# First local-attention layer: keys projected once per head, rope partners by DMA, head sums as two rounded products

## The chip, the cores and the metric

One core of a Trainium2 chip runs the whole program. The metric is the device time of one execution, in microseconds (us); a kernel's number is the median of its runs. The time of the kernel before is 2983.45 us, the median of 3 runs (2982.0 to 2984.66).

## The reference, cut to what matters

The program computes two small networks one after the other on 512 positions of width 1024: a local-attention layer and an RWKV layer, each followed by a gated feed-forward layer, and then a block with three attention branches (called a, b and c in the kernel) and a last feed-forward layer. What the change touches is how queries and keys are made:

```python
def rms_norm(x, g):
    y = xf * lax.rsqrt(jnp.mean(xf * xf, axis=-1, keepdims=True) + NORM_EPS)
    return (y * g.astype(F32)).astype(x.dtype)

# first local layer: 16 query heads, 4 key heads, 4 value heads of 64 columns
qkv = h @ w_qkv
q = rope_slice(rms_norm(q, q_gain), cos, sin, 0)   # norm over each head's 64 columns
k = rope_slice(rms_norm(k, k_gain), cos, sin, 0)   # then columns 0-7 and 8-15 are rotated

def rope_slice(x, cos, sin, start):
    return concat([x1 * c - x2 * s, x2 * c + x1 * s, x[..., start + rot:]])
```

Four query heads share each key head. Branches a, b and c normalise queries and keys in the same way, without the rotation, over 64 columns (a) or 128 (b, c).

## The kernel before, in words

Everything is held with channels on the 128 partitions and positions along the free axis. A weight tile is 1024 x 128 (8 blocks of 128 x 128, 512 KB). SyncE (SP) loads the tiles, in the order in which they are used, into a ring of five buffers (L1508 to L1516), and waits for the buffer's last reader before each load. ScalarE makes a rounded copy of each (the high part, L295), GpSimd (POOL) subtracts it from the original (the low part, L304), and both go into one of three buffers. TensorE then multiplies each of the 8 blocks three times: high by high, high by low, low by high (L1539 to L1541), 24 products of 512 columns into one PSUM bank. Two banks take turns, and a bank is free for the next tile but one when the named reader has read it.

The first local layer multiplies 14 tiles: 8 of queries (two heads each), 4 of keys, 2 of values. Each of the 4 key tiles holds one key head twice, in partitions 0 to 63 and again in 64 to 127, so that either query head of a tile finds its key beside it. `project` (L1599) walks through the tiles; in the middle of tile i it calls `small(i)`, which on TensorE does the small products of tile i-1 and of tile i-2:

- `head_sum` (L1569, the product is L1574) multiplies the squares by a block of ones, in fp32, so that every partition has its head's sum of squares.
- `rope_turn` (L1577, the product is L1583) multiplies by a permutation, in fp32, so that every rotated channel has its partner beside it, in PSUM.

Around them VectorE (DVE) runs `swa_heads` (L2256), for each tile: `scale` takes the bank times the row norm (L2265), then it waits for the inverse root and multiplies (L2285, which posts HN_Q), then `rotate` does the tile before: times cosine (L2272), the permuted rows times sine (L2274), and their sum (L2275). ScalarE does the square (L1862), the next tile's high part (L295), the logarithm and the exponential that make the inverse root (L1869, L1870), in this order. After the last tile, `attend_swa` begins with score products (L1698).

In branches a, b and c the tiles are made by `project` too. ScalarE squares straight from the bank (L1862), `head_sum` comes in the middle of the next tile, ScalarE makes the inverse root, and DVE multiplies the bank by it (L2303). This last operation posts HN_Q, and that frees the bank for the next tile but one. In branch a the attention's output is normalised as well: `turn_out` (L1761) transposes four tiles, with a `head_sum` after each, and nothing else to do between them. GpSimd also scales the position tables there, by L2207 (four operations) before the low parts of the tiles of branch a and by L2219 (three) for each head of branch b.

The splits of activations (L507 on ScalarE, L513 on DVE) and two operations of the feed-forward layers on DVE (L2464 and L2466, both with two inputs in SBUF) are outside the change, and stand in rows below.

Of the kernel before, what the change touches and what calls it, by code (L numbers as in the profile page):

```python
# [15 lines left out]
P = 128  # L16
# [57 lines left out]
def constants():  # L74
# [8 lines left out]
    perm = np.zeros((P, P))  # L83
# [3 lines left out]
    for h in range(2):  # L87
        for i in range(8):
            lo, hi = 64 * h + i, 64 * h + 8 + i
            perm[hi, lo], perm[lo, hi] = -1.0, 1.0  # L90
            cos[lo] = cos[hi] = np.cos(ang[i])
            sin[lo] = sin[hi] = np.sin(ang[i])
    c["perm"], c["cos"], c["sin"] = perm, cos, sin
# [25 lines left out]
CONST_SETS = [["ident", "ones", "blk", "half"], ["perm", "cos", "sin", "band"],  # L119
              ["lane_mask", "diag", "diag_t", "merge", "eye64", "reset"], ["dist", "dist0", "dist1", "dist2"]]  # L120
CONST_W = {"ident": P, "ones": P, "blk": P, "half": 2, "perm": P, "cos": T, "sin": T, "band": 3 * P,
# [28 lines left out]
def build(nc, ctx, x_in, mem_in, w_in, vec_in, row_in, const_in, small_in, x_spill, out):  # L150
# [99 lines left out]
    for name, kts in tile_table():  # L250
        name = swapped.get(name, name)
# [8 lines left out]
    release = {}  # L260

# [25 lines left out]
    def split_high(act, w):  # L287
# [3 lines left out]
        act.wait_ge(ring_full[w % RING], 16 * (w // RING + 1))  # L291
# [57 lines left out]
    M.pts = at(o, 2, 512); o += 1024  # L349
    M.sq = at(o, 2, 512); o += 1024  # L350
# [4 lines left out]
    o += 2 * KT * T - 6 * 1024  # L355
# [15 lines left out]
    B.oT = pair(o, 4, T); o += NBUF * 512  # L371
    B.sq = at(o, 2, 512); o += 1024
# [11 lines left out]
    assert o + 9856 + 896 <= NORM, o  # L384
# [21 lines left out]
    for name, n in [("swa_q", 8), ("swa_k", 4), ("a_q", 4), ("a_k", 4), ("a_o", 4)] + \  # L406
# [3 lines left out]
    HN_SQ, HN_ST, HN_RS, HN_Q, HN_PERM, HN_OUT = (sem(n) for n in (  # L410
        "hn_squared", "hn_summed", "hn_rsqrt", "hn_scaled", "rope_permuted", "rope_done"))
# [21 lines left out]
    for name in ["swa_q", "swa_k"]:  # L433
# [1068 lines left out]
    def _(sp):  # L1502
# [3 lines left out]

        load_x(0)
        load_x(1)  # L1508
        for n, (off_, w) in enumerate(pieces):
# [15 lines left out]
    def _(pe):  # L1525
        def tile(t, rhs, gate=None, mid=None):

            wait_bank(pe, t)
            for p, (b0, n) in zip(pieces_of[t], cut(kts_of[t])):
                pe.wait_ge(w_low, p + 1)  # L1530
                hi, lo = wsplit[p % SPLITS]
                for b in range(n):
# [11 lines left out]
                    if mid and kt == kts_of[t] // 2:  # L1544
                        mid()
# [31 lines left out]
        def rope_turn(H):  # L1577
            pe.wait_ge(HN_Q, H + 1)
            if H == 0:
                pe.wait_ge(rope_full, 16)  # L1580
            if H >= 2:
                pe.wait_ge(HN_OUT, H - 1)
            pe.matmul(psum[4 + H % 2][:, :], kview(kp_swa, 1, "perm"), M.qn[:, H % 2, :], start=True, stop=True) \  # L1583
              .then_inc(HN_PERM, 1)
# [14 lines left out]
        def project(names, rhs, gate=None, first=None):  # L1599
# [4 lines left out]
            def small(i):  # L1604
                if i == 0 and first:
                    first()
                if 1 <= i <= len(seq):
                    name, f, _, width = seq[i - 1]
                    ph = name.split("_")[0]
                    if name in hn:  # L1610
                        head_sum(hn[name] + f, blk if ph in ("swa", "a") else ones, width, ph)
                    else:
                        turn_values(name, f, att(ph).pts[:, (VT[name][0] + f) % 2, 0:width])
                if i >= 2 and seq[i - 2][0].startswith("swa") and seq[i - 2][0] in hn:
                    rope_turn(hn[seq[i - 2][0]] + seq[i - 2][1])
# [4 lines left out]
            small(len(seq) + 1)  # L1620
# [68 lines left out]
        def attend_swa():  # L1689
            pe.wait_ge(HN_OUT, hn["swa_k"] + 4)  # L1690
            lin_banks_left("swa_v")
            for s in range(len(PAIRS) + 4):
                if s < len(PAIRS):
                    i, qb, lo, n = PAIRS[s]
                    if s >= 2:
# [93 lines left out]
        project(["swa_q", "swa_k", "swa_v"], lambda name: h_split, gate=lambda kt: wait_split(pe, "tok0", kt), first=first_norm)  # L1789
# [7 lines left out]
        for t in tiles_of["rw_o"][2:]:  # L1797
# [8 lines left out]
                 after=lambda f: head_sum(hn["a_o"] + f - 1, ones, T, "a") if f else None)  # L1806
        head_sum(hn["a_o"] + 3, ones, T, "a")
# [29 lines left out]
    def _(act):  # L1837
# [7 lines left out]
        def hn_tiles(name, n, group, width=T, src=None):  # L1845
            h0 = hn[name]
            s = att(name)
            for i in range(n):
# [13 lines left out]
                act.activation(s.sq[:, H % 2, 0:width], bank[:, 0:width], ACT.Square).then_inc(HN_SQ, 1)  # L1862
# [192 lines left out]
        norm("tok0")  # L2055
        hn_tiles("swa_q", 8, 64)
        hn_tiles("swa_k", 4, 64)
# [16 lines left out]
        def values(name, width=T):  # L2074
# [3 lines left out]
            copy_tiles(name, lambda k: (B.pts[:, (VT[name][0] + k) % 2, 0:width], P))  # L2078
        hn_tiles("a_q", 4, 64)
# [55 lines left out]
    def _(pool):  # L2135
# [52 lines left out]
        advance("swa_q", "swa_k", "swa_v")  # L2188
# [49 lines left out]
    def _(dve):  # L2238
# [17 lines left out]
        def swa_heads():  # L2256

            tiles = tiles_of["swa_q"] + tiles_of["swa_k"]
            out_ = [M.q[:, i, :] for i in range(KT)] + [M.k[:, i, :] for i in range(4)]
# [7 lines left out]
            def rotate(H):  # L2267
# [3 lines left out]
                tw, d = M.t1[:, H % 2, :], out_[H]  # L2271
                link(dve.tensor_tensor(tw, M.qn[:, H % 2, :], kview(kp_swa, 1, "cos"), ALU.mult))  # L2272
                dve.wait_ge(HN_PERM, H + 1)
                link(dve.tensor_tensor(d, psum[4 + H % 2][:, :], kview(kp_swa, 1, "sin"), ALU.mult))  # L2274
                dve.tensor_tensor(d, d, tw, ALU.add).then_inc(HN_OUT, 1)  # L2275
# [5 lines left out]

# [416 lines left out]
```

## Time and profile before

| what | us |
|---|---|
| median of 3 runs | 2983.45 |
| the profiled execution, its own time | 2986.75 |
| its span (first to last instruction) | 2984.9 |
| TensorE busy (matmul) | 2837.1 |
| VectorE busy | 1422.5 |
| ScalarE busy | 1255.7 |
| GpSimd busy | 1134.4 |

Busy time is summed over the whole span; one engine's instructions are pipelined, so a row of the timeline that starts before the one ahead of it has ended is no mistake. The time from one start to the next start is what an instruction costs its engine. A projection stage lasts from the first product of its first tile to the first score product after it.

### The profile page before, as it was taken

The page shows a single profiled execution, that of the slowest core. Times are in us where ns is not written, and L with a number is a line of the kernel's source. Part 1 is how long each engine was busy: PE and PEld are TensorE (multiplying, and loading weights), DVE is VectorE, ACT ScalarE, POOL GpSimd, SP SyncE. Part 2 cuts the span into 40 slices and gives each one's busy share as a digit, 9 for nine tenths or more (in the row PEclk, how much of TensorE's full clock was granted, in tenths as well). Part 3 has the DMA queues.
Part 4 walks back from the last instruction along what each step waited for, and adds up shares of the span by engine and source line. Part 5 has one row for each costly group of instructions (what it writes and reads, how often), then busy time and mean ns, then how long its engine had stood idle before and what let it go on. Part 6 is the DMA issues. An engine that isn't in the chain of part 4 may idle for free.

```text
span 2984.9 us, 55448 instructions
## 1 busy us (share of the span) xinstructions
PE 2837.1 (95%) x23572; PEld 2227.5 (75%) x23572; DVE 1422.5 (48%) x2550; ACT 1255.7 (42%) x2290; POOL 1134.4 (38%) x631
## 2 busy tenths in 40 slices
PE   7999999989999999989999989899999989999999
PEld 5667888867777777777888866577767777878887
DVE  5665886066757767654888023402221224334420
ACT  4574443234555555544444234434443344432221
POOL 4214444534622323205444452052333342544443
PEclk9999999999999999999999999999999999999999
DMA  4102322222200000002232321032221231322332
GB/s 146 57 16 92 97 94 89 95 92 92 91 17 5 7 7 7 24 18 92 92 96 85 98 86 52 21 118 76 68 82 50 79 102 44 109 92 92 93 94 75
DMA packets 59366, 211.99 MB, mean 71 GB/s; under 512 B 6832, under 2 KB 7088, under 8 KB 58736
## 3 DMA queue, kind: packets, MB, share of 16 engines
q1 hardware_dynamic: 56160, 192.96, 20.5%
q0 software_dynamic: 2384, 14.06, 1.3%
q8 instruction: 188, 3.08, 0.4%
q10 hardware_dynamic: 576, 1.41, 0.2%
q14 instruction: 58, 0.48, 0.0%
HBM read 204.21 MB, written 4.19 MB: 70 GB/s over the span
## 4 chain that ended last, share of the span: by engine, by line
PE 84%; DVE 7%; ACT 5%; issue 2%; POOL 1%; DMA 0%; SPq 0%; DVEq 0%; ACTq 0%; POOLq 0%
PE banks L1539 21%; PE banks L1540 20%; PE banks L1541 20%; PE banks L734 8%; PE banks L1666 2%; PE banks L1574 2%; PE banks L1644 1%; DVE low L513 1%; PE banks L649 1%; DVE arena L2303 1%; ACT arena L1870 1%; ACT arena L1869 1%; PE banks L785 1%; PE banks L727 1%; DVE arena L2437 1%
## 5 line engine op out<-in xcount | busy, mean ns | idle before, releaser
L304 POOL TENSOR_TENSOR low<-arena,high 128x1024 fp32r<-128x1024 f32 (+1 forms) x378 | 879.8, 2329 | 1386.4 <-ACT high L295 1386.2
L1539 PE MATMUL banks<-high,high 128*128 128x512 f32 (+1 forms) x2768 | 1121.3, 405 | 42.2 <-POOL low L304 21.2
L1541 PE MATMUL banks<-high,low 128*128 128x512 f32 (+1 forms) x2768 | 1089.2, 393 | 0.0
L1540 PE MATMUL banks<-low,high 128*128 128x512 f32 (+1 forms) x2768 | 1089.0, 393 | 0.0
L295 ACT ACTIVATE high<-arena 128x1024 fp32r<-128x1024 f32 (+1 forms) x378 | 384.3, 1017 | 825.9 <-PE banks L1541 815.5
L1539 PEld LDWEIGHTS banks<-high,high 128*128 128x128 f32 x2768 | 522.7, 189 | 195.4 <-DVE arena L2303 25.1
L1540 PEld LDWEIGHTS banks<-low,high 128*128 128x128 f32 x2768 | 523.0, 189 | 129.4 <-issue 13.2
L1541 PEld LDWEIGHTS banks<-high,low 128*128 128x128 f32 x2768 | 522.3, 189 | 122.5
L734 PE MATMUL banks<-arena 64*64 64x64 f32 x7680 | 292.0, 223 | 20.2 <-ACT arena L1048 11.7
L734 PEld LDWEIGHTS banks<-arena 64*64 64x64 f32 x7680 | 251.9, 136 | 79.4 <-ACT arena L1048 30.3
L2466 DVE SCALAR_TENSOR_TENSOR arena<-arena 128x511 f32<-128x511 f32 x88 | 239.1, 2717 | 3.1
L2334 DVE TENSOR_TENSOR arena<-banks,arena 128x512 f32<-128x512 f32 x48 | 33.1, 692 | 434.5 <-PE banks L1541 424.5
L1048 ACT ACTIVATE arena<-banks 128x256 f32<-128x256 f32 (+2 forms) x384 | 144.2, 384 | 167.9 <-PE banks L734 158.4
L2490 DVE TENSOR_TENSOR arena<-banks,arena 128x512 f32<-128x512 f32 x132 | 91.3, 692 | 224.8 <-PE banks L1541 222.8
L513 DVE TENSOR_TENSOR low<-arena,high 128x512 fp32r<-128x512 f32 (+1 forms) x142 | 183.6, 1294 | 24.0 <-ACT high L507 22.7
L2303 DVE SCALAR_TENSOR_TENSOR arena<-banks,arena 128x512 f32<-128x512 f32 (+1 forms) x44 | 32.0, 727 | 274.4 <-ACT arena L1870 274.4
L1430 DVE TENSOR_TENSOR arena<-banks,arena 128x128 f32<-128x128 f32 x320 | 88.4, 289 | 147.2 <-PE banks L734 145.1
L1186 POOL TENSOR_TENSOR arena<-arena 128x128 f32<-128x128 f32 x64 | 27.6, 451 | 301.0 <-DVE arena L1456 300.9
L507 ACT ACTIVATE high<-arena 128x512 fp32r<-128x512 f32 (+1 forms) x142 | 86.2, 609 | 42.8 <-DVE arena L1237 27.3
L1869 ACT ACTIVATE arena<-banks,arena 128x512 f32<-128x512 f32 (+1 forms) x56 | 37.6, 672 | 141.2 <-PE banks L1574 141.2
L1883 ACT ACTIVATE arena<-banks 128x512 f32<-128x512 f32 (+2 forms) x48 | 27.8, 578 | 114.6 <-PE banks L1541 84.9
L2029 ACT ACTIVATE arena<-arena 128x512 f32<-128x512 f32 x44 | 27.8, 633 | 101.3 <-DVE arena L2466 101.3
(252 smaller groups left out, 2992.0 us busy)
## 6 DMA issues: line engine op xcount, KB each, us to landing
arena<-weights SPq DMA_DIRECT2D x306, 512.0 KB, 3.5
arena<-weights SPq DMA_DIRECT2D x48, 448.0 KB, 3.2
arena<-weights SPq DMA_DIRECT2D x24, 256.0 KB, 2.6
arena<-tables POOLq DMA_DIRECT2D x13, 448.0 KB, 4.3
arena<-x_t SPq DMA_DIRECT2D x4, 512.0 KB, 8.1
x_spill<-arena POOLq DMA_DIRECT2D x1, 2048.0 KB, 9.2
arena<-small_weights POOLq DMA_DIRECT2D x16, 128.0 KB, 2.7
arena<-x_spill POOLq DMA_DIRECT2D x1, 2048.0 KB, 8.9
```

What stands on the lines that cost most here:

```text
L295: act.activation(wsplit[w % SPLITS][0][:, 0:n], ring[w % RING][:, 0:n], ACT.Copy).then_inc(w_high, 1)
L304: pool.tensor_tensor(lo[:, 0:n], ring[w % RING][:, 0:n], hi[:, 0:n].bitcast(F32), ALU.subtract).then_inc(w_low, 1)
L507: act.activation(dst[0], src((s0 + i) % 2), ACT.Copy).then_inc(act_high, 1)
L513: dve.tensor_tensor(dst[1], src((s0 + i) % 2), dst[0].bitcast(F32), ALU.subtract).then_inc(act_low, 1)
L734: mm = pe.matmul(bank[hf(p), col + C * q:col + C * q + C], lhs(hf(p), q), rhs(hf(p), q), start=True, stop=True)
L1048: a2.inc(act.activation(dst, PJ[h][:, 0:n], ACT.Copy), f"{name}_{h}")
L1430: d2.inc(dve.tensor_tensor(u, PI[h][:, 0:P], u, ALU.add), f"U{s}_{h}")
L1539: pe.matmul(dst, hi[:, c], x[0], start=kt == 0, stop=False)
L1540: pe.matmul(dst, hi[:, c], x[1], start=False, stop=False)
L1541: mm = pe.matmul(dst, lo[:, c], x[0], start=False, stop=kt == kts_of[t] - 1)
L2466: dve.scalar_tensor_tensor(a[:, 0:T - 1], b[:, 1:T], vcol("conv_w", L * 132 + 88 + g * FT + i), a[:, 0:T - 1], ALU.mult, ALU.add).then_inc ...
L2490: dve.tensor_tensor(F.up[:, n % 2, :], bank_of(t), F.rs, ALU.mult).then_inc(up_scaled, 1)
```

## The change

- Keys: two tiles of keys instead of four, each with two different key heads. The load of such a tile ("joined") is made of two DMAs, each of which takes 64 of the 128 columns of a stored tile, in runs of 256 bytes. The rotated halves go to `M.k` by an addition for each half, and four DMAs from SP copy them into the other 64 partitions (`double_keys`).
- Order: keys, queries, values, instead of queries, keys, values. 12 tiles in all.
- Rope: the permutation product is gone. `swap_pairs` on SP moves the 8-row partners with four DMAs a tile, from `M.qn` into `M.pm` in SBUF, after HN_Q of the tile, and is called in the loop of weight loads behind load H+8. The sign is in the sine table. DVE waits for the four DMAs (`rope_moved`). The tables lose the permutation.
- DVE order in `swa_heads`: scale(H), cosines(H-1), square_low(H), sines(H-1), then the wait for the inverse root of H and its product. Before the first, `M.pm` is filled with zeros.
- Head sums, here and in a, b and c: ScalarE copies the square, rounded (high); DVE subtracts it (low); TensorE multiplies both by a rounded block of ones as two rounded (fp32r) products. In the local layer the place in a tile is after block 6 instead of 4. ScalarE rounds the blocks of ones once in the local layer and once ahead of branch a.

```diff
+    for name, kts in [("swa_k", KT)] * 2 + [("swa_q", KT)] * 8 + [(swapped.get(n, n), k) for n, k in tile_table()[12:]]:
         off = stored[name].pop(0)
+        if name == "swa_k":
+            joined[len(pieces)] = stored[name].pop(0)
...
+        def swap_pairs(H):
+            sp.wait_ge(HN_Q, H + 1)
+            if H >= 2:
+                sp.wait_ge(HN_OUT, H - 1)
+            for h in range(2):
+                for e in range(2):
+                    a, b = 64 * h + 8 * e, 64 * h + 8 * (1 - e)
+                    sp.dma_start(M.pm[a:a + 8, H % 2, :], M.qn[b:b + 8, H % 2, :]).then_inc(rope_moved[H % 2], 16)
+
+        def double_keys(i):
+            sp.wait_ge(HN_OUT, hn["swa_k"] + i + 1)
+            sp.dma_start(M.k[64:128, 2 * i, :], M.k[0:64, 2 * i, :]).then_inc(k_doubled, 16)
+            sp.dma_start(M.k[0:64, 2 * i + 1, :], M.k[64:128, 2 * i + 1, :]).then_inc(k_doubled, 16)
...
+            if n in joined:
+                for e, a in enumerate((off_, joined[n])):
+                    sp.dma_start(ring[n % RING].rearrange("p (k c) -> p k c", c=P)[:, :, 64 * e:64 * e + 64],
+                                 w_in[a:a + P * w].rearrange("(p k c) -> p k c", p=P, c=P)[:, :, 64 * e:64 * e + 64]) \
+                      .then_inc(ring_full[n % RING], 16)
+                continue
             sp.dma_start(ring[n % RING][:, 0:w], w_in[off_:off_ + P * w].rearrange("(p w) -> p w", p=P)) \
               .then_inc(ring_full[n % RING], 16)
+            H = n - 8
+            if 0 <= H < hn["swa_q"] + KT:
+                swap_pairs(H)
+            if H in (1, 2):
+                double_keys(H - 1)
...
-            pe.matmul(psum[2 + H % 2][:, 0:width], group, s.sq[:, H % 2, 0:width], start=True, stop=True) \
-              .then_inc(HN_ST, 1)
+            if H in (0, hn["a_q"]):
+                pe.wait_ge(groups_ready, 1 + (H > 0))
+            pe.matmul(psum[2 + H % 2][:, 0:width], group, s.sq_high[H % 2][:, 0:width], start=True, stop=False)
+            pe.matmul(psum[2 + H % 2][:, 0:width], group, s.sq_low[H % 2][:, 0:width], start=False, stop=True).then_inc(HN_ST, 1)
...
-                tile(t, rhs(name), gate if i == 0 else None, lambda: small(i))
+                tile(t, rhs(name), gate if i == 0 else None, lambda: small(i), 6 if name.startswith("swa") and i else None)
...
-                act.activation(s.sq[:, H % 2, 0:width], bank[:, 0:width], ACT.Square).then_inc(HN_SQ, 1)
+                q_ = act.activation(s.sq[:, H % 2, 0:width], bank[:, 0:width], ACT.Square)
+                link(q_)
+                act.activation(s.sq_high[H % 2][:, 0:width], s.sq[:, H % 2, 0:width], ACT.Copy).then_inc(HN_HIGH, 1)
...
+            def square_low(H):
+                dve.wait_ge(HN_HIGH, H + 1)
+                dve.tensor_tensor(M.sq_low[H % 2], M.sq[:, H % 2, :], M.sq_high[H % 2].bitcast(F32), ALU.subtract) \
+                   .then_inc(HN_SQ, 1)
...
+            def sines(H):
+                tw, pm = M.t1[:, H % 2, :], M.pm[:, H % 2, :]
+                dve.wait_ge(rope_moved[H % 2], 64 * (H // 2 + 1))
+                link(dve.tensor_tensor(pm, pm, kview(kp_swa, 1, "sin"), ALU.mult))
+                if H >= nk:
+                    dve.tensor_tensor(M.q[:, H - nk, :], pm, tw, ALU.add).then_inc(HN_OUT, 1)
+                    return
+                dve.tensor_tensor(M.k[0:64, 2 * H, :], pm[0:64], tw[0:64], ALU.add)
+                dve.tensor_tensor(M.k[64:128, 2 * H + 1, :], pm[64:128], tw[64:128], ALU.add).then_inc(HN_OUT, 1)
...
+            link(dve.memset(M.pm, 0.0))
+            dve.wait_ge(N_RS, 1)
             for H in range(len(tiles)):
                 scale(H)
+                if H:
+                    cosines(H - 1)
+                square_low(H)
+                if H:
+                    sines(H - 1)
                 dve.wait_ge(HN_RS, H + 1)
...
             value(0)
-            rotate(len(tiles) - 1)
+            cosines(len(tiles) - 1)
+            sines(len(tiles) - 1)
             value(1)
...
+                if s is B:
+                    dve.wait_ge(HN_HIGH, H + 1)
+                    dve.tensor_tensor(s.sq_low[H % 2][:, 0:width], s.sq[:, H % 2, 0:width],
+                                      s.sq_high[H % 2][:, 0:width].bitcast(F32), ALU.subtract).then_inc(HN_SQ, 1)
                 dve.wait_ge(HN_RS, H + 1)
```

## Rows read from the trace of the kernel before

**Rows 1.** The page, costliest groups: busy us, mean ns, idle before and its releaser.
```profile
L1539 PEld LDWEIGHTS banks<-high,high 128*128 128x128 f32 x2768 | 522.7, 189 | 195.4 <-DVE arena L2303 25.1
```
**Rows 2.** Chain of waits in the local layer: start us, length us, engine, line.
```profile
44.31 0.86 PE banks L1574 x2
45.17 0.86 PE banks L1583 x2
...
51.60 0.86 PE banks L1574 x2
```
**Rows 3.** Timelines of DVE, ACT and POOL, one local-layer tile: start, length, engine, line.
```profile
42.09 0.68 DVE L2265 TENSOR_TENSOR arena<-banks,arena 128x512 f32<-128x512 f32 x1
42.80 0.63 ACT L1862 ACTIVATE arena<-arena 128x512 f32<-128x512 f32 x1 [3.47 <-DVE arena L2265]
43.34 1.04 ACT L295 ACTIVATE high<-arena 128x1024 fp32r<-128x1024 f32 x1
44.46 2.37 POOL L304 TENSOR_TENSOR low<-arena,high 128x1024 fp32r<-128x1024 f32 x1 [6.12 <-ACT high L295]
45.20 0.69 ACT L1869 ACTIVATE arena<-banks,arena 128x512 f32<-128x512 f32 x1 [0.82 <-PE banks L1574]
46.68 0.75 DVE L2285 SCALAR_TENSOR_TENSOR arena<-arena 128x512 f32<-128x512 f32 x1 [3.91 <-ACT arena L1870]
49.41 0.69 DVE L2265 TENSOR_TENSOR arena<-banks,arena 128x512 f32<-128x512 f32 x1
```
**Rows 4.** Timeline, DVE beside POOL: last local tiles, and a feed-forward layer.
```profile
114.99 2.39 POOL L304 TENSOR_TENSOR low<-arena,high 128x1024 fp32r<-128x1024 f32 x1 [2.49 <-ACT high L295]
115.05 0.68 DVE L2280 TENSOR_TENSOR arena<-banks,arena 128x512 f32<-128x512 f32 x1
115.65 2.29 DVE L2272 TENSOR_TENSOR arena<-arena 128x512 f32<-128x512 f32 x1
...
284.28 2.41 POOL L304 TENSOR_TENSOR low<-arena,high 128x1024 fp32r<-128x1024 f32 x1 [3.18 <-ACT high L295]
284.47 2.77 DVE L2466 SCALAR_TENSOR_TENSOR arena<-arena 128x511 f32<-128x511 f32 x1
```
**Rows 5.** Two issues on SP; then, for 60:120 us, a DMA queue and median landings.
```profile
0.72 0.86 SPq L1504 DMA_DIRECT2D arena<-x_t  x2
...
q1 hardware_dynamic: 1263, 4.65, 24.4%
...
arena<-weights SPq DMA_DIRECT2D x9, 512.0 KB, 3.4
...
arena<-x_t SPq DMA_DIRECT2D x4, 512.0 KB, 8.1
```
**Rows 6.** Timeline: first scaled tile, first head sum, first local score products.
```profile
28.08 0.69 DVE L2265 TENSOR_TENSOR arena<-banks,arena 128x512 f32<-128x512 f32 x1
30.40 1.02 PE L1574 MATMUL banks<-arena 128*128 128x512 f32 x2
121.99 1.35 PE L1698 MATMUL banks<-arena 64*128 64x256 f32 x8
```
**Rows 7.** Timeline of branch a: a wait for POOL, then one tile.
```profile
1783.93 0.47 PE L1539 MATMUL banks<-high,high 128*128 128x512 f32 x1 [2.06 <-POOL low L304]
...
1799.15 0.60 ACT L1862 ACTIVATE arena<-banks 128x512 f32<-128x512 f32 x1 [0.65 <-PE banks L1541]
1799.34 0.50 PE L1539 MATMUL banks<-high,high 128*128 128x512 f32 x1 [0.23 <-DVE arena L2303]
1800.77 2.40 POOL L304 TENSOR_TENSOR low<-arena,high 128x1024 fp32r<-128x1024 f32 x1 [4.54 <-ACT high L295]
1802.93 1.02 PE L1574 MATMUL banks<-arena 128*128 128x512 f32 x2
```
**Rows 8.** Timeline: a sum of branch a's output, and the last of branch c.
```profile
1909.45 2.08 PE L1574 MATMUL banks<-arena 128*128 128x512 f32 x2
...
2462.75 1.13 PE L1574 MATMUL banks<-arena 128*128 128x512 f32 x2 [0.69 <-ACT arena L1862]
```

More of the change, by code:

```diff
@@ L260, in build, with ring_fills @@
     release = {}
+    def ring_fills(w):
+        return w // RING + 1 + sum(1 for j in joined if j <= w and j % RING == w % RING)
     piece_done = sem("piece_done")
@@ L354, in build @@
     M.t1 = at(o, 2, 512); o += 1024
-    o += 2 * KT * T - 6 * 1024
+    M.pm = at(o, 2, 512); o += 1024
+    M.sq_high, M.sq_low = ([nc.alloc_sbuf_tensor_at(f"swa_squares_{part}{i}", [P, T], F32R, offset=start + 4 * (a + T * i))[:, :]
+                            for i in range(2)] for part, a in (("high", o), ("low", SWA_SQ_AT)))
+    o += 1024
+    M.blk_r = nc.alloc_sbuf_tensor_at("swa_blk_rounded", [P, P], F32R, offset=start + 4 * o)[:, :]
+    o += P
     assert o <= NORM, o
@@ L383, in build @@
     B.dist = at(o + 9856, 896)
-    assert o + 9856 + 896 <= NORM, o
+    assert o + 9856 + 896 + 1280 <= NORM, o
+    B.sq_high, B.sq_low = ([nc.alloc_sbuf_tensor_at(f"squares_{part}{i}", [P, T], F32R, offset=start + 4 * (a + T * i))[:, :]
+                            for i in range(2)] for part, a in (("high", o + 10752), ("low", SQ_AT)))
+    blk_r, ones_r = (nc.alloc_sbuf_tensor_at(f"{n}_rounded", [P, P], F32R, offset=start + 4 * (o + 11776 + P * i))[:, :]
+                     for i, n in enumerate(("blk", "ones")))
     B.bq = at(o, 3, T)
@@ L409, in build @@
         nh += n
-    HN_SQ, HN_ST, HN_RS, HN_Q, HN_PERM, HN_OUT = (sem(n) for n in (
-        "hn_squared", "hn_summed", "hn_rsqrt", "hn_scaled", "rope_permuted", "rope_done"))
+    HN_HIGH, groups_ready = sem("hn_squares_high"), sem("groups_ready")
+    HN_SQ, HN_ST, HN_RS, HN_Q, HN_OUT = (sem(n) for n in (
+        "hn_squared", "hn_summed", "hn_rsqrt", "hn_scaled", "rope_done"))
     for name, h0 in hn.items():
@@ L432, in build @@
     swa_normed = sem("swa_normed")
-    for name in ["swa_q", "swa_k"]:
+    rope_moved, k_doubled = [sem(f"rope_moved{i}") for i in range(2)], sem("k_doubled")
+    for name in ["swa_k", "swa_q"]:
         for i, t in enumerate(tiles_of[name]):
@@ L1805, in _ @@
         turn_out("a_o", lambda f, q: B.O4[:, q, f * P:(f + 1) * P], 4,
-                 after=lambda f: head_sum(hn["a_o"] + f - 1, ones, T, "a") if f else None)
-        head_sum(hn["a_o"] + 3, ones, T, "a")
+                 after=lambda f: head_sum(hn["a_o"] + f - 1, ones_r, T, "a") if f else None)
+        head_sum(hn["a_o"] + 3, ones_r, T, "a")
         def mix(b, name):
@@ L2055, in _ @@
         norm("tok0")
+        act.wait_ge(loaded, 32)
+        act.activation(M.blk_r, blk, ACT.Copy).then_inc(groups_ready, 1)
+        hn_tiles("swa_k", 2, 64)
         hn_tiles("swa_q", 8, 64)
-        hn_tiles("swa_k", 4, 64)
         for t in tiles_of["swa_v"]:
@@ L2078, in values @@
             copy_tiles(name, lambda k: (B.pts[:, (VT[name][0] + k) % 2, 0:width], P))
+        act.activation(blk_r, blk, ACT.Copy)
+        act.activation(ones_r, ones, ACT.Copy).then_inc(groups_ready, 1)
         hn_tiles("a_q", 4, 64)
@@ L2256, in swa_heads @@
         def swa_heads():
-            tiles = tiles_of["swa_q"] + tiles_of["swa_k"]
-            out_ = [M.q[:, i, :] for i in range(KT)] + [M.k[:, i, :] for i in range(4)]
+            tiles = tiles_of["swa_k"] + tiles_of["swa_q"]
+            nk = hn["swa_q"]
             def scale(H):
```

56 lines of the change are left out of this document (20 added, 36 removed).

## The prediction

> **What bounds the kernel now.** I read the page's busy times first: TensorE has 2837.1 of 2984.9 us. It is the engine to relieve wherever nothing else sets its pace, so the next view is the chain of waits in the stage that changes most. In the local layer the chain never leaves TensorE: a head sum of 0.86 us, a permutation of 0.86, and a head sum again 7.29 us after the first [rows 2]. A tile there is 5.57 us of weight products and 1.72 of small fp32 ones. DVE, ACT and POOL have slack, and the timeline shows how much [rows 3]: scale (42.09) to square is 0.71 us, to the next tile's high part 1.25, to POOL's start 2.37, and POOL then runs 2.37. In branches a, b and c another thing sets the pace: a tile waits a little for DVE's L2303, which frees its bank [rows 1, 7], and that operation follows the head sum through the inverse root. A shorter sum shortens that chain too. The third view is DVE beside POOL, because the change adds DVE work there.
>
> **Two DVE operations under one POOL operation.** POOL runs from 114.99 to 117.38. The DVE operation at 115.05, which reads a PSUM bank and SBUF, takes its usual 0.68 us. The one at 115.65, with two inputs in SBUF, takes 2.29 and ends 0.56 after POOL. In the feed-forward layer it is the same: POOL ends at 286.69, the two-SBUF-input operation at 287.24 [rows 4]. So such an operation that meets a running POOL subtraction is held, and ends 0.55 us after it. The Trainium skill (SBUF — State Buffer, "Who interferes with whom") says this as a rule: a DVE instruction with two SBUF inputs shares a port pair with a GpSimd instruction that reads SBUF, whichever starts first keeps it for the whole instruction, and the other blocks. The trace agrees. If instead each took its own length, the stage would go by the first rival below. The change turns the sine product from a PSUM reader into such an operation, so the rule speaks against it.
>
> **Local layer, TensorE's part.** Two tiles go (2 x 7.29 = 14.6), ten permutations (8.6), and ten sums become two products of 0.23, 0.46 in all, for 0.86 (4.0). TensorE would need 5.57 + 0.46 = 6.03 us a tile.
>
> **Local layer, the loop through DVE.** Scale(H) starts at s. Square at s+0.71; the rounded copy after it, s+1.37 to 2.0; DVE's low part s+2.05 to 2.75, ahead of POOL. The weight tile's high part is now behind the copy, s+1.91 to 2.95, and POOL starts at s+3.03 and ends at s+5.4. The sines of tile H-1 wait for the four partner DMAs. The trace has none like them. An issue costs SP 0.43 [rows 5], so the last goes out 1.4 after HN_Q; landing lies between nothing and the 3.4 of a 512 KB load. I take 2 for 16 KB, so 3.4 us after HN_Q (bounds 1.4 to 4.8), which is s+3.5. A weight load issued 1.9 us before HN_Q lands at about s+1.6 and is out of the way. At s+3.5 POOL has the ports: the sine product ends at 5.4 + 0.55 = 5.95. Then the addition, the product by the inverse root (ready since s+4.9) and the next scale follow at 0.68 each (46.68 to 49.41 is four such steps [rows 3]). The period is 7.3 us, though TensorE needs 6.03. For any landing between s+3 and s+5.3 it stays 7.3; earlier, the sine product slips in front of POOL and the addition is held instead, 7.0.
>
> **Local layer, the sum.** Scale(0) was at 28.08 [rows 6]. The 1024 columns of zeros come in front of it; bounds 0 and two 512-column operations, 1.3; I take 1.1. The joined loads move 2048 runs of 256 bytes each in place of 4 KB rows. Per engine that is 128 runs; at equal cost per byte nothing is added, at the mean of a packet (24.4% of 16 x 60 us over 1263 = 0.185 us [rows 5]) 128 x 0.185 = 23.7, less some 1.6 for the bytes, 22. Loads of x behind the first one carry the start. I take 1.0, near the lower end, because the mean packet is 3.7 KB and its time mostly bytes. The Trainium skill (DMA: Bandwidth & Descriptors, "Why small descriptors are slow (HBM only)") gives 27% overhead at 256 bytes, by which it would be an estimated 0.4. Then s0 = 30.2. The first round has no sines: sum at s0+2.8, root, product, s1 = s0+5.6 = 35.8. Two rounds finish key tiles with one addition more, 8.0 each: 51.8. Six at 7.3: s9 = 95.6. Behind it: POOL starts the next low part at once, before the waiting addition (s9+5.95 to 8.3); product(9) ends at +9.6; its partners land at +13.0, into another POOL subtraction (+12.6 to 15.0); sine, addition, last value tile, its transposes: scores at s9+17.5 = 113.1. Before, 121.99. The local layer gains 8.9, of the 27 that TensorE gives up. Nothing behind it changes: the doubled keys land long before the scores, and SP's waits on HN_Q, with weight loads queued behind them, have five ring buffers of cover.
>
> **Branch b.** 24 sums, each 0.40 shorter. The added copy and subtraction must be done when TensorE comes to the sum, 3.78 us after the square starts (1799.15 to 1802.93 [rows 7]). Copy at +0.66, subtraction +1.3 to 2.05, and POOL's low part, pushed by the copy, at +2.3: on time, and begun 1.0 ahead of POOL. Gain 9.6; the position tables scaled by POOL may hold a subtraction now and then, -0.5: 9.1 (bounds 0 and 9.6).
>
> **Branch a, projections.** Eight sums, but the third tile waits 2.06 us for POOL [rows 7], which hides the first two; 6 x 0.40 = 2.4, less 0.55 where a subtraction pushes POOL: 1.8.
>
> **Branch a, output.** Nothing covers the small steps there. Each sum needs copy and subtraction first, +1.4. A pair of products is 2.08 us there instead of 1.02 [rows 8, 7], so 0.84 is saved on three and 0.4 on the first: 1.0 + 3 x 0.56 = 2.7 lost (bounds 1.5 and 5.6).
>
> **Branch c.** Four sums of 256 columns, 0.2 each, and three of 0.4; the last stands after the last tile and already waits for its square [rows 8], +1.4 - 0.4. Together 1.0 gained.
>
> **Total.** 8.9 + 9.1 + 1.8 - 2.7 + 1.0 = 18.1. The profiled execution took 2986.75 us (span 2984.9), 3.3 above the median; 2986.75 - 18.1 = 2968.65 for its own kind, and 2983.45 - 18.1 = 2965.4 for the median.
>
> **Rivals.**
> - *TensorE keeps the pace in the local layer.* DVE slips its two-SBUF operations past POOL. For it: POOL is busy only 2.37 of 7.3 us. Against it: both rows 4, and POOL starts at a fixed distance from scale. First sum 33.0, nine periods of 6.03, product, partners, sine, addition, value and transposes 8.9: scores at 96.2, another 16.9 gained, 2948.5.
> - *The partner DMAs pace the layer.* They are issued on the queue of the weight loads. With L from HN_Q to the last landing, the period is L + 2.1 once L passes 5.2. At 8.1, as the loads of x take [rows 5], eight rounds lose 2.9 each, 23.2, and the tail some 3.5: 2992, slower. The point from which the whole change loses is L = 5.2 + 18/8 = 7.4. Against it: a quiet queue and 3.4 for 32 times the bytes.
> - *The subtraction comes under POOL in a and b.* POOL starts 1.0 behind it; a DVE later than that is held. Held each time, it ends 5.3 after the square and the sum is 1.5 late: 32 x 1.5 = 48 lost, 3013. Against it: order on ACT is fixed, the copy is ahead of the weight split.
>
> **Chances.** Forecast 0.66, its own range 2960 to 2971. TensorE's pace 0.13. Partners or subtractions late in part, 2968 to 2980, 0.10. Partners at 8 us 0.05, subtractions held 0.04, a loss elsewhere that cancels the gain 0.02. A measurement here can tell 0.2%, some 6 us, from no change. Faster 0.66 + 0.13 + 0.07 = 0.86, same 0.03 + 0.02 = 0.05, slower 0.09. The range that leaves out the slower cases and the very end of the fast one is 2950 to 2977.
>
> **What would show it.** In the new trace: head sums 7.3 us apart in the local layer with TensorE idle about 1.2 us in each; the sine product 2 to 2.5 us long and ending 0.55 after POOL; the first scores near 113; partners landed some 3.4 us after HN_Q. In b the sums 0.40 closer and no wait for the subtraction; in branch a's output sums 0.5 farther apart. Wrong would be: sums 6.0 apart; a sine product that starts only when POOL is long done (late partners); a first weight product many us later than before (joined loads); TensorE waiting for DVE's subtraction in b.

## The result, and the profile after

The changed kernel takes 2965.43 us (median of 4 runs, 2964.81 to 2968.19); the kernel before, beside it on the same chip, 2984.05 (4 runs, 2982.0 to 2984.66). The ratio is 0.9941, 95% interval 0.9923 to 0.9958: faster by 0.6%, 18.6 us, which is small but clear of the spread. Forecast: 2965.4.

| what | before | after |
|---|---|---|
| the profiled execution, its own time | 2986.75 | 2968.19 |
| its span | 2984.9 | 2966.4 |
| TensorE busy (matmul) | 2837.1 | 2793.7 |
| first local layer, to its first score product | 121.99 | 113.31 |
| branch a's projections, first to last product by the inverse root | 51.92 | 50.15 |
| branch a's output, last write of the attention's output to DVE's first product by the gate behind it (four sums and two weight tiles lie in it) | 28.19 | 32.25 |
| branch b, first to last product by the inverse root | 291.54 | 282.64 |
| branch c, the same | 51.79 | 51.08 |

Two lines of the page of the changed kernel. TensorE gave up 43.4 us of work and the span only 18.5: over half of the saved work came back as waits. The idle time ahead of L1581's weight loads fell from 195.4 to 186.1 [rows 1].

```profile
PE 2793.7 (94%) x23496; PEld 2213.7 (75%) x23496; DVE 1466.1 (49%) x2597; ACT 1284.5 (43%) x2339; POOL 1131.7 (38%) x629
...
L1581 PEld LDWEIGHTS banks<-high,high 128*128 128x128 f32 x2752 | 520.5, 189 | 186.1 <-DVE arena L2364 24.9
```

The timeline of one local-layer tile of the changed kernel, the counterpart of [rows 3]: start, length, engine, line; in brackets the idle time before it and what ended it. Here and in the timelines below, rows of other instructions in between are left out.

```profile
66.03 0.68 DVE L2305 TENSOR_TENSOR arena<-banks,arena 128x512 f32<-128x512 f32 x1
66.13 2.65 SPq L1531 DMA_DIRECT2D arena<-arena  x4
67.94 1.04 ACT L299 ACTIVATE high<-arena 128x1024 fp32r<-128x1024 f32 x1
68.14 0.69 DVE L2309 TENSOR_TENSOR swa_squares_low<-arena,swa_squares_high 128x512 fp32r<-128x512 f32 x1 [0.83 <-ACT swa_squares_high L1898]
68.89 0.50 PE L1618 MATMUL banks<-swa_squares_high,swa_blk_rounded 128*128 128x512 f32 x1 [0.98 <-DVE swa_squares_low L2309]
69.06 2.41 POOL L308 TENSOR_TENSOR low<-arena,high 128x1024 fp32r<-128x1024 f32 x1 [4.89 <-ACT high L299]
70.12 1.89 DVE L2321 TENSOR_TENSOR arena<-arena 128x512 f32<-128x512 f32 x1 [1.29 <-DMA arena<-arena]
72.05 0.69 DVE L2323 TENSOR_TENSOR arena<-arena 128x512 f32<-128x512 f32 x1
72.66 0.75 DVE L2343 SCALAR_TENSOR_TENSOR arena<-arena 128x512 f32<-128x512 f32 x1
73.32 0.68 DVE L2305 TENSOR_TENSOR arena<-banks,arena 128x512 f32<-128x512 f32 x1
```

Scale (L2305) is followed by the next scale 7.29 later. POOL runs 69.06 to 71.47, and the sine product (L2321), which takes up 0.69 us of DVE when nothing is beside it, takes 1.89 and ends at 72.01, 0.54 behind POOL. It is the only operation of the loop that takes longer than its usual time. It also starts only when the last partner has landed (1.29 of waiting before it). TensorE stands 0.98 before the head sum at 68.89. The head sums start at 32.22, 38.27, 46.19, 54.30, 61.60, 68.89, 76.18, 83.48, 90.78 and 98.08.

The chain of waits of the next tile of the changed kernel (start, length, engine, line), the counterpart of [rows 2]; pieces of 0.04 and less between these are left out. It has left TensorE: it goes through SP's four issues, the last landing and DVE's two-input product. Up to 75.45 these are the partner issues; the landing at 77.40 still falls inside POOL's subtraction (76.4 to 78.8), which is what ends the sine product.

```profile
73.43 0.63 SPq L1531
74.10 0.64 SPq L1531
74.79 0.62 SPq L1531
75.45 1.95 DMA arena<-arena
77.43 1.90 DVE arena L2321
```

The chain names the DMA as the releaser, and the question that the profile leaves open is whether the DMA or POOL is what must be removed. Half of the experiments are about that.

### The profile page after: what moved, and what is told of

Its sections match the earlier page's. It is cut to its first block, busy times and chain, and to the rows that moved or that the text cites. A ratio compares the mean times of both kernels' runs of the same rounds, so it can differ in the third digit from the quotient of the medians.

```text
span 2966.4 us, 55427 instructions
## 1 busy us (share of the span) xinstructions
PE 2793.7 (94%) x23496; PEld 2213.7 (75%) x23496; DVE 1466.1 (49%) x2597; ACT 1284.5 (43%) x2339; POOL 1131.7 (38%) x629
## 4 chain that ended last, share of the span: by engine, by line
PE 81%; DVE 8%; ACT 6%; issue 2%; POOL 1%; DMA 1%; SPq 1%; DVEq 0%; ACTq 0%; POOLq 0%
PE banks L1581 20%; PE banks L1583 20%; PE banks L1582 20%; PE banks L751 8%; PE banks L1698 2%; PE banks L1676 1%; DVE low L530 1%; PE banks L666 1%; DVE arena L2364 1%; ACT arena L1906 1%; ACT arena L1905 1%; PE banks L802 1%; PE banks L744 1%; DMA arena<-arena 1%; SPq L1531 1%
## 5 line engine op out<-in xcount | busy, mean ns | idle before, releaser
L1581 PE MATMUL banks<-high,high 128*128 128x512 f32 (+1 forms) x2752 | 1094.6, 398 | 44.9 <-POOL low L308 24.1
L1581 PEld LDWEIGHTS banks<-high,high 128*128 128x128 f32 x2752 | 520.5, 189 | 186.1 <-DVE arena L2364 24.9
L2364 DVE SCALAR_TENSOR_TENSOR arena<-banks,arena 128x512 f32<-128x512 f32 (+1 forms) x44 | 32.0, 727 | 158.9 <-ACT arena L1906 158.9
```

The costliest lines, as they stand in the source:

```text
L1581: pe.matmul(dst, hi[:, c], x[0], start=kt == 0, stop=False)
```

## The experiments

Theory: the local layer's period of 7.3 us is set by the sine product behind POOL, not by the partner DMAs; TensorE could do 6.03. The branches gain the shorter sum, except branch a's output, which loses. Rivals: the DMAs set the pace; the whole gain of the branches is drift. Each result is given as a ratio to the kernel before on the same chip. That was 2985.2 beside the first PSUM kernel, both fp32 kernels and the first kernel with both edits; 2985.51 beside the kernels with two and eight partner DMAs, with both together, and with plain key loads; 2983.66 beside the repeats and the last experiment. "Scores" is the start of the first local score product.

**Sine product with only one input in SBUF.** The sines are copied once into a free PSUM bank, and the cosine product goes to PSUM as well.

```diff
+        act.activation(psum[7], kview(kp_swa, 1, "sin"), ACT.Copy).then_inc(sine_ready, 1)
-                link(dve.tensor_tensor(M.t1[:, H % 2, :], M.qn[:, H % 2, :], kview(kp_swa, 1, "cos"), ALU.mult))
+                link(dve.tensor_tensor(psum[4 + H % 2], M.qn[:, H % 2, :], kview(kp_swa, 1, "cos"), ALU.mult))
-                tw, pm = M.t1[:, H % 2, :], M.pm[:, H % 2, :]
+                tw, pm = psum[4 + H % 2], M.pm[:, H % 2, :]
-                link(dve.tensor_tensor(pm, pm, kview(kp_swa, 1, "sin"), ALU.mult))
+                link(dve.tensor_tensor(pm, pm, psum[7], ALU.mult))
```

> The changed kernel, but the sine table stands in a PSUM bank and the cosine product is written to one, so that no rotation operation on VectorE has two inputs in SBUF. Theory (the two-input operations held by GpSimd set the local layer's pace): the sine product starts when its partners land, 4.1 us after scale, and takes 0.7 instead of 1.9; head sums 6.1 us apart instead of 7.3, first scores near 99 instead of 113, 2951 us. Rival (the partner DMAs and SP's issues set the pace): head sums stay 7.3 apart, 2965 us.

One thing in this expectation is wrong: the cosine product itself still reads two SBUF operands (`M.qn` and the cosines). What the edit takes away is the second SBUF input of the sine product and of the addition.

Measured: 2949.67 (2946.91 to 2952.8), ratio 0.9882 (0.9868 to 0.9895); scores at 99.66, head sums 6.1 apart once the key tiles are done. Run once more in the last group, to stand on the same chip as the changed kernel:

> The kernel with the tables in PSUM once more: 2949.7 us and 0.988 if its first measurement stands.

2952.31 (2951.16 to 2954.46), ratio 0.9893 (0.9879 to 0.9906), scores at 99.98. The timeline of the first of the two, one tile and then the last cosine product:

```profile
62.19 0.68 DVE L2309 TENSOR_TENSOR arena<-banks,arena 128x512 f32<-128x512 f32 x1
65.23 2.42 POOL L308 TENSOR_TENSOR low<-arena,high 128x1024 fp32r<-128x1024 f32 x1 [4.25 <-ACT high L299]
66.29 0.69 DVE L2327 TENSOR_TENSOR arena<-arena,banks 128x512 f32<-128x512 f32 x1 [1.30 <-DMA arena<-arena]
68.29 0.69 DVE L2309 TENSOR_TENSOR arena<-banks,arena 128x512 f32<-128x512 f32 x1
...
92.67 2.48 POOL L308 TENSOR_TENSOR low<-arena,high 128x1024 fp32r<-128x1024 f32 x1 [0.64 <-ACT high L299]
93.40 2.30 DVE L2320 TENSOR_TENSOR banks<-arena 128x512 f32<-128x512 f32 x1
```

The sine product starts at the landing, 4.10 behind scale (4.09 in the changed kernel), in the middle of POOL's subtraction as before, and takes 0.69. The cosine product (L2320), with its two SBUF inputs, runs ahead of POOL in nine tiles and takes 0.69 there. The last one comes under POOL, takes 2.30 and ends 0.55 behind it. So in one kernel the product with one input in PSUM is not held and the one with both in SBUF is. The idle time in the groups of 56 to 100 us tells the same. Columns: line, engine, names, count | busy, mean ns | idle before, releaser. First the changed kernel, then this one; TensorE's wait at the head sum goes from 5.9 us in six tiles to 0.2, while DVE's wait for the DMA is 9.7 and 9.4.

```profile
L2321 DVE TENSOR_TENSOR arena<-arena 128x512 f32<-128x512 f32 x7 | 12.6, 1794 | 9.7 <-DMA arena<-arena 9.7
...
L1618 PE MATMUL banks<-swa_squares_high,swa_blk_rounded 128*128 128x512 f32 x6 | 3.0, 497 | 5.9 <-DVE swa_squares_low L2309 5.9
```

```profile
L2327 DVE TENSOR_TENSOR arena<-arena,banks 128x512 f32<-128x512 f32 x7 | 4.8, 688 | 9.4 <-DMA arena<-arena 9.4
...
L1619 PE MATMUL banks<-swa_squares_high,swa_blk_rounded 128*128 128x512 f32 x6 | 2.7, 453 | 0.2 <-DVE swa_squares_low L2313 0.2
```

So the landing, which the chain named, was not what cost: it is as late here, and the layer is 13.7 us shorter. POOL's hold on the two-input product cost those 13.7.

**Half of the partner DMAs.** Only the lower head's partners are moved; the upper head's rotation is left out of the computation.

```diff
-            for h in range(2):
+            for h in range(1):
...
-                dve.wait_ge(rope_moved[H % 2], 64 * (H // 2 + 1))
+                dve.wait_ge(rope_moved[H % 2], 32 * (H // 2 + 1))
```

> The changed kernel with only the two partner DMAs of the lower 64 partitions (the upper heads' rotation is left out), so that they land 2.8 us after scale instead of 4.1. Theory (GpSimd holds): the sine product now starts ahead of the weight tile's low part, and the addition is held instead: head sums 7.0 apart, 2962. Rival (the DMAs set the pace): 6.0 apart, 2952.

2961.81 (2959.33 to 2964.52), ratio 0.9912 (0.9897 to 0.9927), scores at 110.64: as the theory had it. The periods alternate between 7.3 and 6.9. The timeline of DVE and POOL shows why:

```profile
67.94 2.41 POOL L308 TENSOR_TENSOR low<-arena,high 128x1024 fp32r<-128x1024 f32 x1 [4.17 <-ACT high L299]
68.22 2.68 DVE L2321 TENSOR_TENSOR arena<-arena 128x512 f32<-128x512 f32 x1 [0.51 <-DMA arena<-arena]
...
75.24 2.69 POOL L308 TENSOR_TENSOR low<-arena,high 128x1024 fp32r<-128x1024 f32 x1 [4.89 <-ACT high L299]
75.70 2.78 DVE L2323 TENSOR_TENSOR arena<-arena 128x512 f32<-128x512 f32 x1
```

In the first round the sine product starts 0.28 behind POOL and is held to 0.55 past its end. In the next it starts at 74.97, 0.27 ahead of POOL: now DVE keeps its 0.69, POOL's operation is the longer one by 0.28, and the addition behind it (L2323) is held instead, until 78.48, again 0.55 past POOL. In the first of these rounds the data came 0.8 us earlier than in the changed kernel (3.31 behind scale instead of 4.09), in the second the sine product was free to start 1.3 earlier (2.77). Over the whole layer that is worth 2.7 us.

**Both together** (this kernel too leaves out the upper head's rotation).

> Tables in PSUM, and only the two partner DMAs of the lower 64 partitions (the upper heads' rotation is left out). Theory: with the hold gone, the landing 4.1 us after scale sets the 6.1 us; with 2.8 the layer falls to TensorE's own pace, 6.03, first scores near 97.5, 2947.5. Rival (a further wait in the round of squares, sum and root): 6.1 or more, 2949.5 as with four.

2949.68 (2946.26 to 2950.8), ratio 0.9872 (0.9856 to 0.9889), scores at 97.41; sums 6.03 apart, the length of TensorE's own work. Once the operands are in PSUM, two DMAs fewer are worth some 2 us more. DVE is now early: its product waits 0.4 to 0.5 for the inverse root.

**Eight partner DMAs.** Four more of the same size, into a spare buffer, ahead of the four that count; the wait is for all.

```diff
+            for to in (M.spare, M.pm):
                 for h in range(2):
                     for e in range(2):
...
-                dve.wait_ge(rope_moved[H % 2], 64 * (H // 2 + 1))
+                dve.wait_ge(rope_moved[H % 2], 128 * (H // 2 + 1))
```

> The changed kernel with four more partner DMAs a tile, into a spare buffer, issued ahead of the four that count, and all eight waited for. From the profile an issue costs SP 0.66 and the last lands 1.95 after its issue, so they land 7.2 us after HN_Q instead of 4.0. Theory (the wait is free until the sine product would be released by GpSimd anyway, 5.3 us after scale, and sets the period at L + 2.1 beyond it): head sums 9.3 us apart instead of 7.3, 2985 us, about the time of before. Rival (what holds the layer is GpSimd alone): 7.3 apart, 2965.

2981.81 (2977.94 to 2985.26, 9 runs), ratio 0.9985 (0.9975 to 0.9995); scores at 128.35.

```profile
72.41 0.68 DVE L2307 TENSOR_TENSOR arena<-banks,arena 128x512 f32<-128x512 f32 x1
72.52 5.32 SPq L1533 DMA_DIRECT2D arena<-arena  x8
79.18 0.69 DVE L2323 TENSOR_TENSOR arena<-arena 128x512 f32<-128x512 f32 x1 [3.98 <-DMA arena<-arena]
81.18 0.68 DVE L2307 TENSOR_TENSOR arena<-banks,arena 128x512 f32<-128x512 f32 x1
```

The last landing is 6.67 behind HN_Q, and one scale is 8.77 behind the other: L + 2.1, the formula of the rival in the prediction. I had forecast L 7.2 here, so 9.3 us and 2985; the size was off, the formula was not. Here the sine product takes 0.69, because POOL is long done: this is what a pace set by the DMAs looks like, and the changed kernel (1.89, ending with POOL) does not look like it.

**Head sums in fp32 again, in a, b and c.** The local layer stays changed. `plain(H)` holds for all tiles of the branches.

```diff
+            if plain(H):
+                full = blk if group is blk_r else ones
+                pe.matmul(psum[2 + H % 2][:, 0:width], full, s.sq[:, H % 2, 0:width], start=True, stop=True).then_inc(HN_ST, 1)
+                return
...
-                if s is B:
+                if s is B and not plain(H):
```

> The changed kernel with the head sums of branches a, b and c as one fp32 product again; the local layer keeps the change. Theory (each of the parts gained or lost what the profile shows): b gives back 9.3, a's projections 2.2, c 1.0, and a's output wins 4.1: 8.4 in all, 2974 us. Rival (the local layer is the whole gain): 2965 us.

2979.07 (2972.01 to 2981.49, 8 runs), ratio 0.9977 (0.9967 to 0.9987). Its stages in a, b and c are those of the kernel before but for a's output: a 51.96, a's output 29.67 (28.19 before), b 291.56, c 51.84; the local layer (113.34) is that of the changed kernel. So by stage the sums are worth 1.8 + 8.9 + 0.8 in the projections and cost 2.6 in a's output. The median lies 5 above my forecast, and the runs are 9.5 apart (2972.0 to 2981.5); the sum of the stages is 8.9, for 8.4 expected. Which part of the program makes the rest of the median is not shown. That the whole gain of the branches is drift is ruled out by branch b, where the sums alone move the stage from 282.6 to 291.6.

**Only branch a's output in fp32.** `plain(H)` holds for its four tiles.

> The changed kernel with only the four sums of branch a's output as one fp32 product again. Theory (the copy and the subtraction stand uncovered there, and TensorE's lower clock lasts longer behind them): 4.1 us won, 2961 us. Rival (only the uncovered steps count, the clock is lost anyway): 2.7 won, 2962.7. Second rival (a drift of the profile, no cost there): 2965.

2960.97 (2958.97 to 2962.7), ratio 0.9919 (0.9906 to 0.9933); a's output takes 29.02, 3.2 less than in the changed kernel. The timeline of the changed kernel, with two of its sums, and then two stretches of 10 us (stretch, length, busy of PE, PEld, DVE, ACT and POOL with counts, granted clock, DMA share, GB/s):

```profile
1895.52 0.69 DVE L2358 TENSOR_TENSOR squares_low<-arena,squares_high 128x512 fp32r<-128x512 f32 x1 [1.84 <-ACT squares_high L1898]
...
1902.35 0.79 PE L1618 MATMUL banks<-squares_high,ones_rounded 128*128 128x512 f32 x1 [1.42 <-DVE squares_low L2358]
1908.41 0.80 PE L1618 MATMUL banks<-squares_high,ones_rounded 128*128 128x512 f32 x1 [4.85 <-DVE squares_low L2358]
1909.44 0.63 PE L1581 MATMUL banks<-high,high 128*128 128x512 f32 x1
...
1913.28 0.44 PE L1581 MATMUL banks<-high,high 128*128 128x512 f32 x1
```

```profile
1900.00:1910.00 10.00, 3.73 (x10) 2.33 (x10) 3.09 (x5) 5.01 (x9) 0.00 (x0) 0.50 0.00 1
1910.00:1920.00 10.00, 10.00 (x37) 7.70 (x36) 2.24 (x4) 4.46 (x7) 1.29 (x1) 0.83 0.01 2
```

This stage starts 3.3 us earlier in the experiment (last write of the attention's output at 1884.23, for 1887.55), so its counterpart stretches are 3.3 earlier too:

```profile
1896.70:1906.70 10.00, 6.54 (x13) 3.35 (x12) 2.70 (x5) 4.56 (x7) 0.00 (x0) 0.53 0.00 1
1906.70:1916.70 10.00, 10.00 (x44) 7.80 (x43) 1.38 (x2) 3.67 (x4) 3.54 (x2) 1.00 0.17 54
```

In the kernel before the stage starts at 1897.76. One of its stretches, and its fourth weight product:

```profile
1910.00:1920.00 10.00, 6.54 (x16) 3.40 (x15) 2.70 (x4) 4.57 (x7) 0.00 (x0) 0.60 0.00 0
1918.08 0.39 PE L1539 MATMUL banks<-high,high 128*128 128x512 f32 x1
```

With the two products TensorE waits 1.42 for the subtraction at the second and the third sum, and 4.85 before the last. The granted clock is at the lower of the two levels (0.50, 1.2 GHz) all through 1900 to 1910, and the weight products behind the output begin at that level. The stretch 1910 to 1920 has 0.83, so the lower level lasts to about 1913.4. Nine weight products start 0.43 apart up to 1913.28, and 0.23 apart from then on. In the kernel before the stretch 1910 to 1920 has 0.60, the lower level lasts to about 1918.0, and three weight products run at it. The six more cost 6 x 0.20 = 1.2 us. With fp32 in the changed kernel six run at it (0.53 in the stretch 1896.7 to 1906.7, so to about 1906.1). These three more than before cost 0.6, and as the sums are the same as before there, they don't explain it.

**Both edits together**, the sine operands in PSUM and fp32 in a's output, in two groups:

> Tables in PSUM as in the first of these kernels, and fp32 sums for branch a's output. Theory (the two are in different stages and add up): 14 and 4 us, 2947 us. Rival (one of them is given back further on): the better of the two alone, 2951.

2949.89 (2946.84 to 2950.39), ratio 0.9879 (0.9864 to 0.9894). The stages add up (scores 100.27, a's output 29.16), but the median is that of the first kernel of the same group, 2949.67: 3 us were not to be seen there. Hence once more, beside the changed kernel itself:

> The changed kernel once more, unaltered, beside the three others on one chip. 2965.4 us and a ratio of 0.994 to before if its first measurement stands; the stages between the first local scores and branch a, which the change does not touch, may differ by some us from one execution to the next.

> Tables in PSUM and fp32 sums for branch a's output once more, on one chip with the kernel without these sums. Theory (the stage of branch a's output is 3.1 us shorter in the profile, and nothing gives it back): 3 us under the kernel with the tables alone. Rival (given back further on, as the equal medians of the first measurement say): equal.

The changed kernel: 2967.24 (2966.34 to 2968.31), ratio 0.9942 (0.9929 to 0.9956), scores 113.36, a's output 32.57. With both edits: 2945.70 (2944.4 to 2948.28), ratio 0.9871 (0.9857 to 0.9885), scores 99.80, a's output 29.17. That is 21.5 apart, and 6.6 below the kernel with the PSUM edit alone, where the stage gives 3.1. The two profiled executions are 4.6 apart. A stretch that no edit touches, from the first scores to branch a's first product by its inverse root, is 1646.0 to 1652.6 us long in these profiles, so a few us between two kernels can be spread alone; that the rest here is spread is likely and not shown.

**Key tiles by plain loads.** Each key load is two DMAs of contiguous halves of the first stored tile, so the second head of each key tile holds other numbers.

```diff
-                for e, a in enumerate((off_, joined[n])):
+                for e in range(2):
```

> The changed kernel with each joined key load (runs of 256 bytes from two stored tiles) replaced by two loads of 2 KB runs of the first tile alone (the keys of the second head of a tile are then wrong). Theory (short runs cost nothing that the start waits for, as the first head sum at 32.2 us says): first products and first head sum within 0.5 us of the changed kernel. Rival (the 1.0 us of the prediction): both 1 us earlier.

One execution: 2968.18, scores at 113.89, no gain. The timeline of the changed kernel, then of this one:

```profile
1.64 2.43 SPq L1548 DMA_DIRECT2D arena<-weights  x2
4.12 4.53 SPq L1521 DMA_DIRECT2D arena<-x_t  x2
17.90 0.80 PE L1581 MATMUL banks<-high,high 128*128 128x512 f32 x1 [17.90 <-POOL low L308]
28.36 0.91 DVE L2333 MEMSET arena<- 128x1024 f32 x1 [0.28 <-DVE arena L2581]
29.31 0.69 DVE L2305 TENSOR_TENSOR arena<-banks,arena 128x512 f32<-128x512 f32 x1
```

```profile
1.63 1.09 SPq L1548 DMA_DIRECT2D arena<-weights  x2
2.77 1.07 SPq L1521 DMA_DIRECT2D arena<-x_t  x2
17.98 0.79 PE L1581 MATMUL banks<-high,high 128*128 128x512 f32 x1 [17.98 <-POOL low L308]
29.40 0.69 DVE L2305 TENSOR_TENSOR arena<-banks,arena 128x512 f32<-128x512 f32 x1
```

The runs of 256 bytes cost SP 1.34 us more for the two issues of the first key tile, and the two issues of x behind them took 4.53 instead of 1.07. None of it reaches the start: the first product is at 17.9 or 18.0 either way, and scale(0) at 29.3 or 29.4. The first head sum is at 32.99 here, 0.77 later than in the changed kernel and so outside the 0.5 expected, but later and not earlier; a kernel without this edit (the first with both edits) has it at 33.06.

**The head sum one block earlier in a, b and c** (after block 3 of the next tile instead of block 4), on top of both edits. In branch b of the changed kernel the sums are 6.55 apart, though TensorE's work is about 6.0 a tile; the rest is the wait for L2364, which frees the bank and comes behind the sum.

```diff
-                tile(t, rhs(name), gate if i == 0 else None, lambda: small(i), 6 if name.startswith("swa") and i else None)
+                tile(t, rhs(name), gate if i == 0 else None, lambda: small(i), (6 if name.startswith("swa") else 3) if i else None)
```

> Tables in PSUM and fp32 sums for branch a's output, and in branches a, b and c the head sum comes after block 3 of the next tile instead of after block 4. Theory (a tile there waits half a us for the operation that frees its bank, 6.53 us a tile where TensorE needs 6.03, and the squares' low part is ready 2.3 us into the tile, ahead of 2.8): sums 6.03 us apart in branch b, 12 us won there and some 3 in a and c, 2933 us. Rival (the low part is not ready so early, TensorE waits for it instead of for its bank): nothing won, 2948.

2937.83 (2931.94 to 2939.04), ratio 0.9839 (0.9824 to 0.9855): the fastest of all, 1.6% below the kernel before. Branch b takes 274.44 (282.64 in the changed kernel), a 48.61, c 48.99. I had expected 12 in b; 8.2 came. The timeline of this kernel in branch b tells where the rest is:

```profile
1977.63 0.39 PE L1629 MATMUL banks<-squares_high,ones_rounded 128*128 128x512 f32 x1
1979.84 7.51 POOL L2276 TENSOR_SCALAR arena<-arena 128x896 f32<-128x896 f32 x3
1982.37 1.47 DVE L2377 TENSOR_TENSOR squares_low<-arena,squares_high 128x512 fp32r<-128x512 f32 x1 [1.85 <-ACT squares_high L1912]
1983.90 0.50 PE L1629 MATMUL banks<-squares_high,ones_rounded 128*128 128x512 f32 x1
```

Where POOL does only low parts, the sums are 6.03 apart. Where it scales the position tables (L2276), the subtraction, with two inputs in SBUF, is held for 1.47 instead of 0.69, and the sums there are 6.1 to 6.6 apart. With the sum at its old place there is time enough for that; one block earlier there is none.

## Why the prediction was right

The total was forecast at 18.1, and 18.6 (medians) or 18.5 (profiled executions) came. The terms, by stage, sum to 8.7 + 1.8 - 4.1 + 9.3 + 0.7 = 16.4, which is 1.7 less than forecast. The other 2.1 lie almost wholly behind branch c (519.46 to 517.17), where nothing was changed; this stretch is 515.9 to 519.1 long in the kernels made from the changed one. So an error of 1.7 and a difference of executions of 2.1 cancelled, and that part of the hit is luck. The mechanism of the main term, the local layer, is not.

- **DVE under POOL, local layer.** Forecast: sine product held to 0.55 behind POOL, sums 7.3 apart, scores 113.1. Measured: 0.54, 7.29, 113.31. The product was 1.89 long, just under the forecast 2 to 2.5, because its data came 0.6 later. That this is the cause and not only a coincidence in time is shown by the PSUM experiment (6.1 apart, 99.66) with the landing unchanged. The rule of the Trainium skill (SBUF — State Buffer, "Who interferes with whom"), that whichever of the two starts first keeps the port pair for the whole instruction, agrees with the run with two partner DMAs in both orders: behind POOL the sine product took 2.68 instead of 0.69, ahead of it POOL took 2.69 instead of 2.41.
- **The rival of TensorE's own pace** (6.03 a tile, 2948.5) did not come in the changed kernel. With one operand in PSUM it nearly did: 6.1 a tile and 2949.7 or 2952.3, 1 to 4 us above its 2948.5.
- **Partner DMAs.** An issue costs SP 0.66, not the 0.43 taken from the loads of x, and the last lands 4.0 behind HN_Q (forecast 3.4, bounds 1.4 to 4.8). That is s+4.1, where s is the start of scale. It did not matter, because the prediction's period is the same for any landing between s+3 and s+5.3. The formula L + 2.1 was borne out by the eight DMAs. By it the changed kernel has an estimated 1.2 us (5.2 - 4.0) in hand before the DMAs set the pace.
- **Start.** The joined loads were to cost 1.0. The first product is 0.69 later than before (17.90 for 17.21), but with plain loads it is no earlier (17.98), so the short runs are not the reason, and what is stays open. Scale(0) does not show it: DVE's operation ahead of the zeros ends at 28.08, where scale(0) itself began before. The zeros take 0.91 and 0.28 of waiting ahead of them, and scale(0) came at 29.31, 1.2 later than before for a forecast of 2.1 (30.2). From scale to scale the first round then took 5.92 instead of 5.6, the two key rounds 8.1 each for 8.0, and the last tail 18.1 for 17.5. These errors cancel, which leaves the forecast for the scores right to 0.2.
- **Branch b.** 8.9 in the stage and 0.4 ahead of it, 9.3 for 9.1; the sums are 6.55 apart where they were 6.93. By its timeline, in some tiles the subtraction takes 0.95 instead of 0.69, and the sum still comes in time.
- **Branch a, output: the mis-sized term.** "1.0 + 3 x 0.56 = 2.7 lost" was 4.1. The steps are as forecast: 0.80 a product at the lower clock, the sums 6.1 apart, 1.42 of waiting, and the product by the inverse root of the fourth tile 2.8 later behind the last write (23.60 for 20.82). What the sum put at nothing is what comes behind: nine weight products of the next tile run at the lower granted clock instead of three, and that is the other 1.2. This stage is 29.02 to 29.34 long in the four kernels with fp32 here and two-product sums elsewhere, and 29.67 in the one with fp32 in all branches. So the two products cost 2.6 to 3.2 of the 4.1; the rest, 0.8 to 1.5, stays with fp32 too. In the first of these kernels six weight products instead of three run at the lower clock; why is not shown.
- **Branches a and c.** 1.8 for 1.8, and 0.7 for 1.0. The first is in part luck: in the repeat of the changed kernel branch a's projections took 51.27, a gain of only 0.7, and in other kernels with the same code there 48.3 to 50.1.

## What to carry to other kernels

When work moves from TensorE to DVE, look first at where its operands lie: an operation with two inputs in SBUF that starts under a POOL operation like these ends half a microsecond behind it, and the chain of waits names the DMA or the semaphore that came before it, not POOL. PSUM banks for one operand of the sine product and of the addition gave 15 us here (2967.24 against 2952.31 on one chip), nearly as much as the whole change. A cheaper TensorE product that needs two small steps more is a gain only where other work stands in between; where nothing does, keep the single one.

## What the runs showed that was not expected

- These small DMAs between parts of SBUF (8 partitions, 16 KB) are paced by their issue: 0.66 us of SP each (2.65 for four, 5.32 for eight), and the last lands 1.95 after its issue began.
- The first two loads in runs of 256 bytes took 2.43 us of SP's issue instead of 1.09, and the two loads of x behind them 4.53 instead of 1.07, but the first product was not later for it.
- When DVE is ahead by 0.27 us, POOL's operation is the one that takes longer (2.69 instead of 2.41) and the next DVE operation waits for it; both orders cost about the same.
- Executions differ by several us in stretches that no edit touches (1646.0 to 1652.6), so that an edit worth 3 us is to be read from its stage, not from one group's medians. A stage can have its own spread too: branch a's projections took 48.3 to 51.3 with the same code, branch b 282.6 to 282.7.
